# Hyena convolution: the first inverse in rows of time, with the gate transposed ahead of it, and loads behind scatters

## What is computed

```python
u = short_conv(h @ w_in + b_in, conv_w, conv_b)
x1, x2, v = jnp.split(u, 3, axis=-1)
z = v
for n, gate in enumerate((x1, x2)):
    z = gate * bidir_long_conv(z, filt[:, n, 0], filt[:, n, 1], fbias[n])
return z @ w_out + b_out
# bidir_long_conv: irfft(rfft(z, 2L) * rfft(k, 2L), 2L)[:L] + z * bias, k the two-sided filter
```

## Time and profile before

| | us |
|---|---|
| median of 3 runs | 3555.58 (3554.17 to 3557.77) |
| the profiled execution, its time | 3557.13 |
| its span, first to last instruction | 3555.5 |
| PE busy | 3246.7 |
| DVE busy | 2162.5 |
| ACT busy | 1286.1 |
| POOL busy | 312.9 |
| longest kind of idle time of PE in the convolutions: until DMA for L2452 | 27.4 in four waits |

### The profile page before, as it was taken

How to read it: one execution, slowest core, us unless ns; L and a number is a source line. 1 busy time by engine, 2 the same in 40 slices (tenths; PEclk the granted TensorE clock), 3 DMA queues, 4 the chain that set the end, 5 groups by cost and what they waited for, 6 DMA issues and landing times.

```text
span 3555.5 us, 49957 instructions
## 1 busy us (share of the span) xinstructions
PE 3246.7 (91%) x19458; PEld 2554.6 (72%) x19458; DVE 2162.5 (61%) x3209; ACT 1286.1 (36%) x2121; POOL 312.9 (9%) x508
## 2 busy tenths in 40 slices
PE   7999888988698999998999889999999979999897
PEld 4888545655476888887788667777778758887685
DVE  6998654444466555454768556555556576655676
ACT  3112333333344333332445433333334253333344
POOL 0111234444200000000000200000000000000000
PEclk8999999999899999999999999999999989999999
DMA  7555656567702322224434310000002133333532
GB/s 293 203 200 201 212 150 168 138 180 180 231 25 67 114 92 86 84 83 186 151 96 164 122 53 10 8 7 7 7 25 78 48 113 104 101 107 118 213 99 88
DMA packets 183696, 410.14 MB, mean 115 GB/s; under 512 B 33263, under 2 KB 60207, under 8 KB 180791
## 3 DMA queue, kind: packets, MB, share of 16 engines
q1 hardware_dynamic: 131288, 270.56, 22.9%
q0 software_dynamic: 51936, 131.27, 12.6%
q10 hardware_dynamic: 288, 5.77, 0.4%
HBM read 262.38 MB, written 81.00 MB: 97 GB/s over the span
## 4 chain that ended last, share of the span: by engine, by line
PE 74%; DVE 13%; DMA 6%; ACT 3%; issue 3%; POOL 1%; SPq 1%; DVEq 0%; ACTq 0%; POOLq 0%
PE ps L655 19%; PE ps L657 19%; PE ps L656 19%; PE ps L2518 3%; PE ps L2452 2%; PE ps L2491 2%; PE ps L2470 2%; PE ps L2351 2%; PE ps L725 1%; DVE mx L2907 1%; DMA t2z<-s 1%; PE ps L2553 1%; DMA traw<-hidden_scratch 1%; DMA t2k<-s 1%; DMA wraw<-in_w_in 1%
## 5 line engine op out<-in xcount | busy, mean ns | idle before, releaser
L655 PE MATMUL ps<-HB,gsp 128*128 128x512 f32 x1232 | 487.9, 396 | 38.7 <-DVE HB L831 21.9
L656 PE MATMUL ps<-HB,gsp 128*128 128x512 f32 x1232 | 484.2, 393 | 0.0
L657 PE MATMUL ps<-HB,gsp 128*128 128x512 f32 x1232 | 483.2, 392 | 0.0
L1109 DVE TENSOR_TENSOR gsp<-graw,gsp 128x512 fp32r<-128x512 f32 x330 | 226.4, 690 | 262.3 <-ACT gsp L1088 261.5
L1088 ACT ACTIVATE gsp<-graw 128x512 fp32r<-128x512 f32 x330 | 206.5, 628 | 325.6 <-PE ps L657 266.5
L655 PEld LDWEIGHTS ps<-HB,gsp 128*128 128x128 f32 x1232 | 234.0, 190 | 92.4 <-issue 21.4
L655 PE MATMUL ps<-tsp,wdh 128*128 128x512 f32 x616 | 243.6, 395 | 35.6 <-DVE tsp L1366 35.6
L657 PEld LDWEIGHTS ps<-HB,gsp 128*128 128x128 f32 x1232 | 233.7, 190 | 49.7
L656 PEld LDWEIGHTS ps<-HB,gsp 128*128 128x128 f32 x1232 | 234.1, 190 | 46.4 <-issue 1.0
L656 PE MATMUL ps<-tsp,wdh 128*128 128x512 f32 x616 | 241.4, 392 | 0.0
L657 PE MATMUL ps<-tsp,wdh 128*128 128x512 f32 x616 | 241.2, 392 | 0.0
(11 more groups left out here) (279 smaller groups left out, 7446.0 us busy)
## 6 DMA issues: line engine op xcount, KB each, us to landing
graw<-in_w_gu SPq DMA_DIRECT2D x176, 256.0 KB, 2.7
mring<-in_mod_w POOLq DMA_DIRECT2D x78, 512.0 KB, 4.5
hidden_scratch<-R SPq DMA_DIRECT2D x154, 256.0 KB, 2.4
traw<-hidden_scratch SPq DMA_DIRECT2D x154, 256.0 KB, 2.6
t2k<-s POOLq DMA_DIRECT2D x80, 256.0 KB, 5.6
t2z<-s POOLq DMA_DIRECT2D x160, 128.0 KB, 4.6
t2w<-w POOLq DMA_DIRECT2D x160, 128.0 KB, 3.2
wd<-in_w_dx SPq DMA_DIRECT2D x6, 2816.0 KB, 14.3
```

The costliest lines, as they stand in the source:

```text
L655: pe.matmul(o, wh, xh, start=start, stop=False, skip_group_check=onto)
L656: pe.matmul(o, wh, xl, start=False, stop=False, skip_group_check=onto)
L657: return pe.matmul(o, wl, xh, start=False, stop=stop, skip_group_check=onto)
L1109: dve.tensor_tensor(gsp[U % 3][:, 1, :], graw[:, q, W_SLOT[i], :], gsp[U % 3][:, 0, :].bitcast(F32), ALU.subtract).then_inc(w.lo, 1)
```

## The change

It takes the first inverse of each round (B0) and the transposes of its result (Z1) apart and puts them together in another way. A new step **G** follows S1: the gate in `gbuf` is transposed (16 transposes) and copied by DVE to `zbuf`. A new step **Y** stands in the place of B0 and Z1: the inverse is computed with `f1i` as the stationary operand, 64 columns of weights, and `t2w` as the moving one (8 matmuls of 64x512, in pairs that write the upper and lower half of the partitions), so the result has time on the partitions, as the transposes gave it. DVE multiplies it by the transposed gate straight into `zsb`, and the forward stage follows.

Around it:

- SP loads the second gate and the next v together, after all of Y's scatters have landed. The first two tiles of `R` are loaded at the last M0, the other tiles without waiting for `t2w`'s scatters; `mi` is loaded before the last store of `u`.
- S0 uses the banks 6/7 and 4/5 instead of 4/5 and 6/7, and its first group doesn't wait for the third copy of Z by ACT. ACT does S's first `kk` copy ahead of the outstanding copy of a forward stage.
- On DVE the last mods stand ahead of S0's copies, and the modulations behind K3 of rounds 2, 3 and 4 (made during rounds 1 to 3).

```diff
         STEPS += [("M", it, 0), ("S", it, 1)]
+        STEPS += [("G", it, 0)]
         STEPS += [("K", it + 1, 0), ("K", it + 1, 1)] if more else []
-        STEPS += [("B", it, 0)]
-        STEPS += [("Z", it, 1)]
+        STEPS += [("Y", it, 1)]
         STEPS += [("K", it + 1, 2), ("K", it + 1, 3)] if more else []
...
-        SETS_C, SETS_D, SETS_S = ((4, 2), (0, 6)), ((6, 0), (4, 2)), (4, 6)
+        SETS_C, SETS_D, SETS_S = ((4, 2), (0, 6)), ((6, 0), (4, 2)), ((6, 4), (4, 6))
...
+            sp.wait_ge(p_in.full, 24 * 6)
+            sp.dma_start(mi[:], a["k_mi"][:, 0]).then_inc(s_ci, 16)
             store_u(23, 1)
             sp.wait_ge(s_us[0], 12 * 32)
             sp.wait_ge(s_us[1], 12 * 32)
-            sp.wait_ge(p_in.full, 24 * 6)
-            sp.dma_start(mi[:], a["k_mi"][:, 0]).then_inc(s_ci, 16)
...
+                elif kind == "Y" and it < NCH:
+                    sp.wait_ge(s_ae, A_END["Y", it, 1])
+                    sent(sp, B_END["Y", it, 1])
+                    sp.dma_start(share(gbuf, it), u_share(it, 1)).then_inc(s_gl, 16)
+                    sp.dma_start(share(zbuf, it + 1), u_share(it + 1, 2)).then_inc(s_zl, 16)
...
+                    if it == NCH:
+                        sp.wait_ge(s_ae, K_DONE[2 * NCH - 1])
+                        sp.wait_ge(s_bf, KB_AT[-1] + 1)
+                        for k in range(2):
+                            sp.dma_start(R[:, k, :], a["x_t"][:, k, :]).then_inc(s_x2, 16)
...
             sp.wait_ge(s_pr, N_Z)
-            sp.wait_ge(s_w1a, 32 * (N_Z // 8))
-            sp.wait_ge(s_w1o, 32 * 7 * (N_Z // 8))
-            for k in MIX_FIRST[0][:KD - 1]:
+            for k in (3, 2, 4, 5, 6):
                 sp.dma_start(R[:, k, :], a["x_t"][:, k, :]).then_inc(s_x2, 16)
...
+                elif kind == "G":
+                    pe.wait_ge(s_gl, 16 * (2 * it + 1))
+                    for u in range(4):
+                        au = n["A"] + u
+                        bank_a_free(au)
+                        transposes(gbuf, it, u, au)
+                        if u == 1:
+                            forward_held(2)
+                elif kind in "ZY":
+                    if kind == "Y":
+                        pe.wait_ge(s_w1a, 32 * (n["d"] // 8))
+                        pe.wait_ge(s_w1o, 32 * 7 * (n["d"] // 8))
...
+                        if kind == "Z":
+                            transposes(zbuf, it, u, au)
+                        else:
+                            for c2 in range(2):
+                                mm = pe.matmul(ps[rows64(c2), A_BANK[au], :], f1i[:, which, :], inverse_rows(it, u, c2),
+                                               start=True, stop=True)
+                            mm.then_inc(s_af, 1)
                         if u or not lag:
-                            forward_held(len(held) - (lag // 2 if o or u < 3 else 0))
+                            forward_held(len(held) - (lag // 2 if u < 3 else 0))
                         held.append(("Z", au, n["B"] + u, 8 * it + 4 * o + u, which))
                 elif kind == "S":
                     sent(pe, B_END["K", it, 3])
-                    pe.wait_ge(s_be, n["B"] - 1)
                     for u in range(4):
+                        if u == 1 - o:
+                            pe.wait_ge(s_be, n["B"] - 1)
...
-            MODULATED = {("S", 1, 0): (0, 0, 3), ("S", 1, 1): (1, 1, 0), ("S", 2, 0): (2, 1, 3)}
+            MODULATED = {(2, 3): (0, 0, 3), (3, 3): (1, 1, 0), (4, 3): (2, 1, 3)}
...
+                elif kind == "G":
+                    for u in range(4):
+                        au = n["A"] + u
+                        dve.wait_ge(s_af, au + 1)
+                        dve.tensor_copy(zbuf[:, 512 * u:512 * u + 512], bank(A_BANK[au])).then_inc(s_ae, 1)
...
+                            dve.tensor_tensor(zsb[zu % 2][:], bank(A_BANK[au]), zbuf[:, 512 * u:512 * u + 512], ALU.mult
+                                              ).then_inc(s_ae, 1)
```

More of the change, by code:

```diff
@@ L1716, in build @@
             WALK.append((kind, it, o, dict(n)))
-            for x in range(n["A"], n["A"] + 4 if kind in "KZB" else 0):
+            for x in range(n["A"], n["A"] + 4 if kind in "KZGYB" else 0):
                 u = x - n["A"]
@@ L1917, in _ @@
                         filter_load(it + 2)
[L1918 to L1921, removed]
+                elif kind == "G" and it == NCH:
+                    sp.wait_ge(s_kf, n["k"])
+                    for h in range(2):
+                        sp.dma_start(mix_raw[0][:, 4 * h:4 * h + 4, :],
+                                     z_dram[4 * h:4 * h + 4, :, 0:512].rearrange("m p t -> p m t")).then_inc(s_x[h], 16)
+                elif kind == "Y" and it < NCH:
[3 more added lines that the diff above has]
+                    sp.dma_start(share(zbuf, it + 1), u_share(it + 1, 2)).then_inc(s_zl, 16)
                 elif kind == "M" and o == 0:
@@ L2152, in _ @@
                     done = quarter
+                elif kind == "S":
+                    act.wait_ge(s_pr, 8 * (2 * it + o))
+                    for u in (0, 2):
+                        act.wait_ge(s_kf, n["k"] + u + 1)
+                        act.activation(kk[:, 1024 * u:1024 * u + 1024].rearrange("p (a r c) -> p r a c", a=2, r=2),
+                                       pair(SETS_S[o][0]).rearrange("p r (a c) -> p r a c", a=2), ACT.Copy).then_inc(s_ke, 1)
+                        for b in range(taken, n["B"]):
+                            sent_out(b)
+                        taken = n["B"]
                 else:
@@ L2159, in _ @@
                         ahead += 1
-                if kind == "Z":
+                if kind in "ZY":
                     for u in range(4):
@@ L2164, in _ @@
                         taken = n["B"] + u
[L2165 to L2171, removed]
+                if kind == "M":
                     tail = it == NCH and o == 1
@@ L2369, in forward_held, with transposes, inverse_rows @@
                 del held[:count]
+            def transposes(of, it, u, au):
+                for v, n2 in enumerate(signal_phases(it, u)):
+                    at, step = (n2, NBX) if it < NCH else (2 * L_C * u + n2, NBC)
+                    mm = pe.transpose(ps[:, A_BANK[au], P * v:P * (v + 1)], of[:, at:at + step * (P - 1) + 1:step], ident[:])
+                mm.then_inc(s_af, 1)
+            def inverse_rows(it, u, c2):
+                if it < NCH:
+                    return t2w[:].rearrange("p (c j v x) -> p j v c x", c=2, j=4, v=2)[:, u, :, :, P * c2:P * (c2 + 1)]
+                return t2w[:].rearrange("p (c v m x) -> p m v c x", c=2, v=2, x=P)[:, 2 * u + c2]
             held = []
@@ L2789, in _ @@
                         last_mods(LAST_MODS[2 * o - 4:2 * o - 2])
+                    if (it, o) in MODULATED:
+                        modulations(*MODULATED[it, o])
                 elif kind == "S":
+                    if it == 0 and o == 0:
+                        last_mods(LAST_MODS[4:])
                     dve.wait_ge(s_pr, 8 * (2 * it + o))
```

54 lines of the change are left out of this document (19 added, 35 removed).

## The result

| | before | after |
|---|---|---|
| device time, median | 3556.68 us (3554.17 to 3558.34, 4 runs) | 3519.91 us (3517.75 to 3521.71, 4 runs) |
| ratio to before | | 0.9897 (95%: 0.988 to 0.9914) |
| profiled execution / its span | 3557.1 / 3555.5 us | 3520.4 / 3518.7 us |

A forecast was written before the change was run, and what follows sets the result against it. The prediction took TensorE's (PE) chain of waits, 74%, as the bound, its losses in the convolution stage. Terms 28.7 + 5.4 + 8.4 + 9.4 + 8.7 + 9 = 69.6 us gave 3486 us, range 3468 to 3520.

The forecast's parts named there:

- Part 1: G and Y replacing B0 and Z1: Y's first forward transform at 704.5 for 707.62, though K1 starts 4.1 us late.
- rival (c): Y's matmul pairs run one after another, 3.4 us more in five rounds: 3503 us; chance 0.07.
- Part 2: Loads behind Y's scatters: landing falls to 3.9 us, M1 gains 5.4 in round 2; sum 28.7 (18 to 36).
- rival (b): Y's scatters land no sooner, 6.8 instead of 3.9, because K1's scatters ahead are the load: 3503 us; chance 0.13.
- Part 3: PE keeps its full clock at M1 after gaps of some 3.4 us: 1.8 in rounds 0 to 2, 5.4 us.
- Rival (a): PE's clock falls in every round between S1 and K1, with G's transposes not counting as busy: 3500 us; chance 0.25.
- Part 4: S0's waits for copies shrink, B1 starts 2.1 us earlier in rounds 1 to 4: 8.4 us (4 to 9).
- Part 5: Modulations leave S for behind K3 on DVE, hidden by the gap before M1: 9.4 us (6 to 10).
- Part 6: Start: last mods earlier 6.5, mi out of the way 3.2, first gate load beside Z0's scatters 1.0 back: 8.7 (4 to 11).
- The two other terms: At the start: last mods run during S0's wait for scatters, 6.5 us; table mi no longer loaded among those scatters, 3.2.
- Part 7: Tail: R leaves earlier, so PE's 13.24 us wait for a weight tile shrinks: 9 us (2 to 13).
- Rival (d): The value load comes too late and Z0 waits on it, slower: 3572 us at a 40 us landing; chance 0.03.

The follow-up runs named there:

- b1: Kernel before, with only the gate and value loads moved behind the last scatters of Z1: 3548.14 us, ratio 0.9975.
- g2: Changed kernel, with G moved behind K0 and K1 (order K0, K1, G, Y): 3501.57 us, ratio 0.9839.
- c2: Changed kernel, with G behind K0 and K1, first gate load behind first Z0's scatters, R behind M1's last scatters, fourth output-projection weight tile ahead of them: 3487.86 us.
- a1: Changed kernel, with K2's scatters held on POOL until all of Y's have landed, rounds 0 to 2 only: 3519.68 us, ratio 0.9891.
- a4: Changed kernel, with the first gate load (1 MB, round 0) held until the first Z0's scatters have landed: 3515.58 us, ratio 0.9884.
- a3: Changed kernel, with R's last five tiles again waiting for M1's last scatters: 3514.67 us, ratio 0.9883.
- a9: Changed kernel, with R's last five tiles behind M1's last scatters and the output projection's fourth weight tile loaded ahead of them: 3508.77 us, ratio 0.9865.
- a2: Changed kernel, with the gate load back right behind G and the value load right behind Y's products, not waiting for scatters: 3536.33 us, ratio 0.9945.
- a7: Changed kernel, with the last modulation products back behind S0's copies of round 0: 3522.14 us, ratio 0.9901.

## Why the prediction was only half right

The prediction had the mechanism of most parts right. It failed where it took the landing of Y's scatters from a step with other neighbours, and in the tail, where it put the new load beside scatters that PE waits for.

- **Part 1, G and Y: right.** K1 at 692.8 and the first forward transform at 704.8 (forecast 692.8 and 704.5). Y's two pairs took 1.87 us for the 1.7 assumed, so the pairs do run side by side, and rival (c) is out. POOL started 2.4 us sooner (2.5).
- **Part 2, loads behind scatters: the step that failed.** "The landing thus falls to the 3.9 of the step without loads" holds in round 2 where the scatters of K1 are 2.4 to 6.0 us ahead (b1, g2: 3.6 and 3.7, the last 4.2 and 4.7), and not at 0.3 (4.9, the last 6.8). Part 1 had itself worked out that G pushes K1 back by 4.1 us and that Y comes 3 sooner; the same two moves bring their scatters together on POOL (2.2 and 2.4 us measured there, against an old pause of 4.9), and I didn't carry them there. That was rival (b), whose reason was right and to which I gave 0.13, against it only the 3.9 of a step with no quarter ahead. Its price of 3 us in four rounds fits: M1's start gained 2.5, 4.5, 2.4 and 2.1 us in rounds 0 to 3 for 4.6, 8.3, 5.4 and 5.5, 12 us less in all. A smaller slip lies beside it: M1 waits for the last scatter, and 3.9 is the median. From POOL's last issue to M1 round 2 took 6.8 us, but 4.5 in b1 and 4.9 in g2 as well.
- **Part 3, the clock: not gained.** The gaps stayed at 4.93 to 8.68, and M1's first group took 1.99 each time. Whether 3.4 would have kept the clock stays open. It was kept after 3.36 and 2.78 in b1 (rounds 1 and 2), and after 2.27 in c2. In g2 it fell after 2.76, 2.85 and 2.46, only later: the first 16 records took 1.49 to 1.21 and the next 16 took 3.31 to 3.60 for 1.93, some 1.8 us in all. The same holds for 3.96 in a1 (1.09, then 3.31). So the length of the gap alone doesn't decide it, a first group at full rate proves nothing, and my step from one row of 2.77 was worth little. Rival (a) did not happen: after G's 16 transposes with gaps of 0.86, 0.88 and 1.33, K1's 8 records took 1.09. The Trainium skill's rule (TensorE: Matmul & The Clock Gate, Part 4: PE-mode transpose) that transposes don't count as busy, taken as a reason for a fall here, is not borne out by this trace; G is 2.6 us of transposes and no run here had a longer stretch.
- **Part 4, S0: right**, 8.7 for 8.4. **Part 5, modulations: right**, 8.9 for 9.4 in the trace; undoing them alone cost 7.5.
- **Part 6, the start: 6.2 for 8.7** in this trace, 7.7 on average in eight. The term that was mis-sized is the first gate load "beside Z0's scatters: 1.0 back". It cost 4.3 (a4). The two other terms must then have given more than their 9.7: with the gate load late the start gained 12.2 (a4). No run takes the early `mi` back alone, so how they share it stays open.
- **Part 7, the tail: -2.8 for 9, the wrong sign.** "Counting bytes, the queue is empty when B1 ends" was right about the bytes. I put "B1's scatters now share the engines" only into the bound, and B1 waits on just those. The last of them landed after 8.4 us, for 3.6 in a3. A stall of 4.13 and 6.5 us of half rate ate the whole gain. With R in its old place behind the scatters, and the weight tile first, the tail gave 8.2 us in a9, over the stretch in which the changed kernel lost 2.8, about what the term had promised; but that needs the weight tile early, which the change doesn't do, and with R alone in its old place it gave 3.4 (a3).
- **Rival (d)** didn't happen: no gap before Z0 in the changed kernel.

## What to carry to other kernels

When a step is moved, write down for every queue it feeds what now stands directly ahead of it and behind it, not only when it starts: in round 2, 2 us of pause between two batches of scatters took 2.1 us off the last landing (g2), taking two 1 MB loads away 3.5 us (b1). A load that is sent early to fill idle DMA engines must not share them with the transfer that the critical engine waits for next; send the small tile that is needed first, then wait for the scatters, then send the bulk. And a table of steps leaves free choices (G ahead of, between or behind two others) that differ by 18 us with the same instructions: try them.

## What was unexpected of the hardware

- Sixteen scatters of 128 KB issued in 9.4 us landed in a median of 3.6 to 4.1 us when the preceding scatters were issued 2.4 us or more before (b1, g2, c2, rounds 1 and 2), in 3.9 to 5.8 when 0.3 before, and in 7.0 when two 1 MB loads ran as well (a2). The two loads alone, with a pause of 4.9 ahead, gave 6.0.
- One 1 MB load beside the last four scatters raised the slowest landing from 5.0 to 9.0 us.
- The same code shows gaps before M1 that differ by 2 us and more from one profiled execution to another (changed kernel, a4, a9, a3 and a7, which are equal there: 6.04, 6.34, 5.65, 4.23 and 5.83 in round 1; 5.73, 5.77, 6.18, 6.98 and 3.45 in round 2). A single gap is no measure of an edit; four rounds and the median time are.
- A half-rate stretch began behind a stall of 2.46 us (g2) and was absent behind one of 3.36 (b1). It can begin after the first group: after 3.96 (a1) the first 16 records ran at full rate and the next 16 did not. A shorter stall can cost more clock than a longer one: in round 1 the half-rate stretch behind M1's start cost some 3 us after 3.79 (a1) and 1.4 after 6.04 (changed kernel).
